# Expert layer of a decoder: picks translated in bf16, a product moved to ScalarE, and other steps for routing and turn

## The reference, cut to what matters

```python
def peer(xn, w_q, sub_keys, u, v):
    q = (xt @ w_q).reshape(T, PEER_HEADS, 2, PEER_HALF)
    s = jnp.einsum('thpc,hpnc->thpn', q, sub_keys).astype(jnp.float32)
    s1, i1 = lax.top_k(s[:, :, 0], PEER_TOPK)
    s2, i2 = lax.top_k(s[:, :, 1], PEER_TOPK)
    cand = (s1[..., :, None] + s2[..., None, :]).reshape(T, PEER_HEADS, PEER_TOPK * PEER_TOPK)
    cidx = (i1[..., :, None] * PEER_N_KEYS + i2[..., None, :]).reshape(T, PEER_HEADS, PEER_TOPK * PEER_TOPK)
    top_s, top_j = lax.top_k(cand, PEER_TOPK)
    expert = jnp.take_along_axis(cidx, top_j, axis=-1)
    gate = jax.nn.softmax(top_s, axis=-1).astype(xn.dtype)
    ...
        h = jax.nn.gelu(jnp.einsum('cd,chkd->chk', xc, u[ec]), approximate=False)
        return jnp.einsum('chk,chkd->cd', gc * h, v[ec])
```

## Time and profile before

| | us |
|---|---|
| median of 3 runs (3453.45 to 3467.33) | 3453.63 |
| profiled execution, its own time | 3456.26 |
| its span | 3454.4 |
| PE busy | 3285.0 (95%) |
| DVE busy | 2666.9 (77%) |
| ACT busy | 1400.3 (41%) |
| POOL busy | 1126.0 (33%) |
| mean granted clock of PE | 0.973 |

### The profile page before, as it was taken

The page is one execution under the profiler, slowest core; times in us unless marked ns, Lnnn a source line. Parts: engine busy times, 40 slices in busy tenths (PEclk is TensorE's granted clock), DMA queues, the critical chain, the costliest instruction groups (busy, mean ns, idle before and its releaser), DMA issues. The chain is left out here.

```text
span 3454.4 us, 49213 instructions
## 1 busy us (share of the span) xinstructions
PE 3285.0 (95%) x18534; PEld 2920.1 (85%) x18534; DVE 2666.9 (77%) x5415; ACT 1400.3 (41%) x2205; POOL 1126.0 (33%) x666
## 2 busy tenths in 40 slices
PE   7988999999999999998999998999999999999997
PEld 6866899999998788886978876799989998788886
DVE  4664799898976888885457875699898976788886
ACT  3333245545453333332435544234545453333332
POOL 1311363423312464450000001354342422466561
PEclk9988999999999999999999998999999999999999
DMA  4102358878889999993222212348888789999995
GB/s 163 62 7 91 123 170 294 290 268 292 274 315 345 389 389 388 379 384 133 96 74 74 74 44 80 122 131 287 286 272 283 274 312 338 392 391 390 388 390 204
DMA packets 324349, 833.65 MB, mean 241 GB/s; under 512 B 26001, under 2 KB 160657, under 8 KB 320017
## 3 DMA queue, kind: packets, MB, share of 16 engines
q1 hardware_dynamic: 250384, 562.04, 46.3%
q0 software_dynamic: 73728, 268.47, 21.4%
HBM read 721.30 MB, written 109.10 MB: 240 GB/s over the span
## 5 line engine op out<-in xcount | busy, mean ns | idle before, releaser
L1959 ACT ACTIVATE peer_hi<-peer_raw 128x1024 fp32r<-128x1024 f32 x540 | 570.5, 1057 | 651.9 <-PE p_bank L1933 358.6
L2173 DVE TENSOR_TENSOR peer_lo<-peer_raw,peer_hi 128x1024 fp32r<-128x1024 f32 x434 | 532.3, 1227 | 339.4 <-ACT peer_hi L1959 339.1
L1862 POOL DMA_INDIRECT p_grow<-in_u_rows,p_expert x256 | 329.6, 1287 | 758.4 <-DVE p_hid L2181 744.3
L1862 POOL DMA_INDIRECT p_grow<-in_v_rows,p_expert x256 | 452.3, 1767 | 362.9 <-DVE p_acc L2190 315.0
L1933 PE MATMUL p_bank<-peer_hi,p_w_hi 128*128 128x512 f32 x1536 | 478.4, 393 | 3.7 <-DVE peer_lo L2173 3.6
L1933 PE MATMUL p_bank<-peer_lo,p_w_hi 128*128 128x512 f32 x1536 | 478.5, 393 | 0.0
L1933 PE MATMUL p_bank<-peer_hi,p_w_lo 128*128 128x512 f32 x1536 | 478.2, 392 | 0.0
L1884 PE MATMUL p0r_h_ps<-peer_x_hi,peer_hi 128*128 128x384 f32 (+1 forms) x1152 | 401.9, 349 | 11.9 <-ACT p_h_sb L1973 6.6
L1884 PE MATMUL p1r_h_ps<-peer_x_hi,peer_hi 128*128 128x384 f32 (+1 forms) x1152 | 401.3, 348 | 10.0 <-ACT p_h_sb L1973 6.5
L1884 PE MATMUL p0r_h_ps<-peer_x_lo,peer_hi 128*128 128x384 f32 (+1 forms) x1152 | 395.4, 343 | 0.0
L1884 PE MATMUL p1r_h_ps<-peer_x_lo,peer_hi 128*128 128x384 f32 (+1 forms) x1152 | 395.1, 343 | 0.0
(11 more groups left out here) (365 smaller groups left out, 5806.5 us busy)
## 6 DMA issues: line engine op xcount, KB each, us to landing
peer_raw<-in_u SPq DMA_DIRECT2D x256, 512.0 KB, 5.0
peer_raw<-in_v SPq DMA_DIRECT2D x256, 512.0 KB, 10.6
hiddens<-p_h_sb SPq DMA_DIRECT2D x256, 192.0 KB, 3.4
p_w_raw<-hiddens SPq DMA_DIRECT2D x64, 768.0 KB, 10.1
p_g_sb<-gates SPq DMA_DIRECT2D x64, 768.0 KB, 14.0
gates<-x SPq DMA_DIRECT2D x12, 2048.0 KB, 9.5
ba_w<-in_w_b_mix SPq DMA_DIRECT2D x38, 512.0 KB, 3.7
peer_raw<-in_w_peer_q SPq DMA_DIRECT2D x32, 512.0 KB, 4.0
```

The lines of the kernel that those rows point to most:

```text
L1862: pool.indirect_dma_start(out=grow[:, g % RG, :], out_offset=None, in_=table, in_offset=bass.IndirectOffsetOnAxis(ap=expert[:, at:at + 1], ...
L1959: act.activation(hi[:, n % NH, :], raw[:, n % NR, :], ACT.Copy).then_inc(hi_ready, 1)
L2173: dve.tensor_tensor(lo[:, m % NH, :], raw[:, m % NR, :], hi[:, m % NH, :].bitcast(F32), ALU.subtract).then_inc(lo_dve, 1)
```

## The change

Four things change in `peer_stage`. The table of picks and its factors become bf16, and are built by one comparison, eight products and a tree of sums for each of the two sides. The product of `same` with the first part of the gates goes from DVE to ACT, eight activations a batch with one token's gate as the scale. That part is kept in fp32 (`piece0`). Routings of tiles 2 and 3 start 33 blocks after the one before, instead of 35. The turn comes one block later behind its routing, the cut and the one-hots as before.

```diff
-    route_step = [LIST_END, LIST_END + 8, LIST_END + 43, LIST_END + 78]
+    route_step = [LIST_END, LIST_END + 8, LIST_END + 41, LIST_END + 74]
...
     def turns_after(t):
-        return route_step[t] + 9
+        return route_step[t] + ROUTE_PIECES + 1
 
     def cut_step(t):
-        return route_step[t] + 10
+        return turns_after(t) + 1
 
     def hot_step(k):
 
-        return route_step[1 + k // TILE_BATCHES] + 11 + (k % TILE_BATCHES) * 7 // 5
+        return cut_step(1 + k // TILE_BATCHES) + (k % TILE_BATCHES) * 7 // 5
...
-            best_f = early.sb("best_f", [P, NQ, TOPK])
-            table = early.sb("table", [P, TOPK * HK])
+            best_b = early.sb("best_b", [P, NQ, TOPK, 2], BF16)
+            place_b = early.sb("place_b", [P, 2, HK], BF16)
+            table = early.sb("table", [P, 2 * HEADS * CANDS])
...
-            hit = table[:, :].rearrange("p (c k) -> p c k", k=HK)
+            hit = table[:, 0:TOPK * HK // 2].bitcast(BF16).rearrange("p (c k) -> p c k", k=HK)
...
                 def place_gates(k):
                     pe.wait_ge(rows_ready, k + 1)
-                    pe.wait_ge(cols_ready, (k + 1) * PIECES)
+                    pe.wait_ge(cols_ready, (k + 1) * (PIECES - 1))
+                    pe.wait_ge(first_cols, k + 1)
...
+                def weigh_columns(k):
+                    if k % TILE_BATCHES == 0:
+                        act.wait_ge(done, k // TILE_BATCHES + 1)
+                    act.wait_ge(equal, k + 1)
+                    if k >= 2:
+
+                        act.wait_ge(multiplied, (k - 1) * BATCH)
+                    for v in range(BATCH):
+                        at = k * BATCH + v
+                        ins = act.activation(cols[:, k % 2, 0, v // 2, :, v % 2], same[:, v // 2, :, v % 2], ACT.Copy,
+                                             scale=piece0[:, at:at + 1])
+                    ins.then_inc(first_cols, 1)
+
...
+                    if n - 1 in hots_at:
+                        weigh_columns(hots_at[n - 1])
                     if n in place_at:
                         move_gates(place_at[n])
...
                     for s in range(2):
-                        place = pos_f[:, 3 * s, :].rearrange("p (h k) -> p h k", k=TOPK)
-                        for c in range(TOPK):
-                            step.mark(dve.scalar_tensor_tensor(
-                                out=hit[:, c, :].rearrange("p (h k) -> p h k", k=TOPK), in0=place, scalar=float(c),
-                                in1=best_f[:, s:NQ:2, c:c + 1].broadcast_to(by_head), op0=ALU.is_equal, op1=ALU.mult))
+                        step(dve.tensor_tensor(hit.rearrange("p c (k b) -> p c k b", b=2),
+                                               place_b[:, s, :].rearrange("p (k b) -> p k b", b=2).unsqueeze(1)
+                                               .broadcast_to(pairs),
+                                               iota2[:, 0:TOPK, :].unsqueeze(2).broadcast_to(pairs), ALU.is_equal))
+                        for a in range(HEADS):
+                            mine = hit[:, :, a * TOPK:(a + 1) * TOPK].rearrange("p c (k b) -> p c k b", b=2)
+                            step.mark(dve.tensor_tensor(
+                                mine, mine, best_b[:, 2 * a + s, :, :].unsqueeze(2).broadcast_to([P, TOPK, TOPK // 2, 2]),
+                                ALU.mult))
                         step.wait()
                         yield
-                        step(dve.tensor_reduce(pick[:, s, :], hit[:, :, :].rearrange("p c k -> p k c"), AX.X, ALU.add))
+                        n = TOPK // 2
+                        while n > 1:
+                            step(dve.tensor_tensor(hit[:, 0:n, :], hit[:, 0:n, :], hit[:, n:2 * n, :], ALU.add))
+                            n //= 2
+                        step(dve.tensor_tensor(pick[:, s, :], hit[:, 0, :], hit[:, 1, :], ALU.add))
...
                     if k:
 
-                        dve.wait_ge(cols_ready, k * PIECES)
+                        dve.wait_ge(cols_ready, k * (PIECES - 1))
+                        dve.wait_ge(first_cols, k)
...
-                    for c in range(PIECES):
-                        dve.tensor_tensor(cols[:, k % 2, c, :, :, :], same[:, :, :, :], per_token(pieces, c, k),
+                    for c in range(PIECES - 1):
+                        dve.tensor_tensor(cols[:, k % 2, c + 1, :, :, :], same[:, :, :, :], per_token(pieces, c, k),
                                           ALU.mult).then_inc(cols_ready, 1)
```

More of the change, by code:

```diff
@@ L1728, in peer_stage @@
             places = early.sb("places", [P, 2, SD], BF16)
-            pieces = early.sb("pieces", [P, PIECES, SD], BF16)
+            piece0 = early.sb("piece0", [P, SD])
+            rounded = early.sb("rounded", [P, P], BF16)
+            pieces = early.sb("pieces", [P, PIECES - 1, SD], BF16)
             qT = early.sb("qT", [P, 2, S])
@@ L1771, in peer_stage @@
          cut, done, equal, rows_ready, cols_ready, multiplied, g_moved, weighted, w_hi_ready, w_lo_ready, x_loaded,
-         xrow_ready, indexed, used, hidden, weighed, added, gain_loaded, x_stored) = [st.sem(s) for s in (
+         xrow_ready, indexed, used, hidden, weighed, added, gain_loaded, x_stored, first_cols) = [st.sem(s) for s in (
              "hi_ready", "lo_pool", "lo_dve", "summed", "taken", "keys_loaded", "scored", "listed", "own", "shift_done",
@@ L2056, in route @@
                 def route(t):
-                    step.mark(dve.tensor_copy(best_f[:, :, :], best_at[:, t, :, :]))
+                    step.mark(dve.tensor_copy(best_b[:, :, :, :],
+                                              best_at[:, t, :, :].unsqueeze(3).broadcast_to([P, NQ, TOPK, 2])))
                     for first, n_a, n_b in ((0, FULL, TOPK), (FULL, TOPK - FULL, FULL)):
@@ L2101, in route @@
                     step(dve.tensor_tensor(pos_f[:, 1, :], pos_f[:, 1, :], flat_f[:, :], ALU.mult))
-                    step.mark(dve.tensor_tensor(pos_f[:, 0, :], pos_f[:, 0, :], pos_f[:, 1, :], ALU.add))
+                    step.mark(dve.tensor_tensor(place_b[:, 0, :], pos_f[:, 0, :], pos_f[:, 1, :], ALU.add))
                     step(dve.tensor_tensor(pos_f[:, 2, :], pos_f[:, 2, :], flat_f[:, :], ALU.mult))
-                    step(dve.tensor_tensor(pos_f[:, 3, :], pos_f[:, 3, :], pos_f[:, 2, :], ALU.add))
+                    step(dve.tensor_tensor(place_b[:, 1, :], pos_f[:, 3, :], pos_f[:, 2, :], ALU.add))
@@ L2135, in cut_gates @@
                     at, gates = slice((t - 1) * P, t * P), t_ps[:, 2 * P:3 * P]
-                    dve.tensor_copy(pieces[:, 0, at], gates).then_inc(cut, 1)
+                    before = (t - 1) * 5
+                    if t > 1:
+                        dve.wait_ge(cut, before)
+                    dve.tensor_copy(rounded[:, :], gates).then_inc(cut, 1)
                     dve.tensor_copy(places[:, :, at], t_ps[:, 0:2 * P].rearrange("p (a b) -> p a b", b=P))\
                         .then_inc(cut, 1)
-                    dve.wait_ge(cut, t * 4 - 2)
-                    dve.tensor_tensor(left[:, :], gates, pieces[:, 0, at], ALU.subtract).then_inc(cut, 1)
-                    dve.wait_ge(cut, t * 4 - 1)
-                    dve.tensor_copy(pieces[:, 1, at], left[:, :]).then_inc(cut, 1)
-                    dve.wait_ge(cut, t * 4)
-                    dve.tensor_tensor(pieces[:, 2, at], left[:, :], pieces[:, 1, at],
+                    dve.wait_ge(cut, before + 2)
+                    dve.tensor_copy(piece0[:, at], rounded[:, :]).then_inc(cut, 1)
+                    dve.tensor_tensor(left[:, :], gates, rounded[:, :], ALU.subtract).then_inc(cut, 1)
+                    dve.wait_ge(cut, before + 4)
+                    dve.tensor_copy(pieces[:, 0, at], left[:, :]).then_inc(cut, 1)
+                    dve.wait_ge(cut, before + 5)
+                    dve.tensor_tensor(pieces[:, 1, at], left[:, :], pieces[:, 0, at],
                                       ALU.subtract).then_inc(done, 1)
```

3 lines of the change are left out of this document (2 added, 1 removed).

## The result

The changed kernel took 3427.78 us, the median of 6 runs (3424.97 to 3437.35). The kernel before, run beside it, took 3460.12 (3453.45 to 3467.33). The ratio is 0.9913, with a 95% interval of 0.9892 to 0.9934: faster by 23 to 37 us. Executions of one kernel differ by 12 to 14 us, so the profiled one of the changed kernel (3435.57 us, span 3433.8) is only 20.6 us shorter in its span than the profiled one of before.

What follows compares the result with a forecast made beforehand. PE, busy 95% of the span, bounds the kernel; only its waits and slow clock can shrink. 26.2 + 7.3 = 33.5, less 1 allowed, gives 32.5 us: 3423.8 as profiled, 3421 median; range 3411 to 3440.

Steps and rivals of the forecast that it cites:

- the 33.5 us that were to go at the turns: PE's chain at the turns: 26.2 us of waits plus 7.3 us of slow-clock blocks behind them were to go.
- The waits on the gate: PE's transposes at the turns wait for a routing's gates, 26.2 us over both expert layers; forecast to end.
- A side: One of a routing's two halves on DVE: new operations 4.8 us instead of 7.17, saving 2.4 a side, 4.8 a routing.
- R2: Rival: ACT's strided activations cost 0.45 us each, ACT becomes the bound, 39 us added, 3460 us; chance 0.10.
- R1: Rival: routing no shorter, POOL's lowerings block the new two-input DVE operations; gain 18 to 26 us, say 3431; chance 0.20.
- With 4.8 us gained and the blocked time unchanged: DVE's routings: with the later turn, all four long waits end 1.7 to 3.7 us before PE comes.
- The waits of tile 1: PE's two waits at tile 1's turns, 1.8 us together, under 1 us each, were to end too.
- Behind the turn are late only the cut of the gates and the first one-hot, in DVE's next block: DVE's queue behind the turn: PE needs these only three blocks further, so the deadline moves the full 4.16 us.
- the spacing and ACT's product at nothing: Routings 33 blocks apart, and DVE's 66 us of products moved to ACT: both costed at no change in time.
- the long waits: PE's four waits at the turns before token tiles 2 and 3: 5.92, 5.25, 5.92 and 7.30 us, all to end.
- R3: Rival: in routings ACT's late take and exponential table loads meet in one block, up to 11.6 us, 3433; chance 0.08.
- The start of the weighing: Moves 4 blocks ahead, same distance to the last store of gates; its stall was to stay as it is.

Runs made afterwards that it cites:

- the split store: Changed kernel with each 2 MB store of gates sent as four 512 KB transfers in four successive blocks: 3431.71 us, 0.9929; same edit on the kernel before: 3455.34 us, 0.9992.

## Why the prediction was right, and where not

The forecast was 32.5 us less; the medians give 32.3, the ratio 30, and the two profiled executions 20.6 in their spans. The size is right and the list of causes is not, since two terms were too large and two that stood at nothing were not. That they made up for each other is luck: the 33.5 us that were to go at the turns are 25.1 in the table (37.2 to 12.1), and without the spacing, which was put at nothing, the gain is 16 us.

*Right.* The waits on the gate went to nothing. A side costs what was forecast where nothing disturbs it: the rest of a routing fell by 4.4 us, against 4.8. ACT's activations take 0.310 us against 0.307, hot blocks keep their pace, and R2 did not come. The Trainium skill, SBUF — State Buffer, section Who interferes with whom, had the side of R1: two-input DVE instructions wait for the whole of a GpSimd instruction that reads SBUF, tensor_reduce does not; the sums of 1.47 us that took 6.28 and the reductions that kept 3.88 agree. In the routing of tile 2 before, only the first reduction had a lowering beneath it (the second starts at 698.03, and the last lowering ends at 694.46), so by that rule 2.4 of the 4.8 us go, and they did.

*Wrong: "With 4.8 us gained and the blocked time unchanged".* Picks save 2.0 us a routing at tiles 2 and 3 (50.9 to 49.0, 50.6 to 48.4), since the blocked time rose by one lowering. This is R1's mechanism at half its price; waits of its size are there, but on DVE's lowering and not at the transposes. The waits of tile 1, which were to end, became longer by the picks. In the whole change they can't be told from nothing: 0.9922 without them, 0.9913 with them, the intervals overlap.

*Wrong: "Behind the turn are late only the cut of the gates and the first one-hot, in DVE's next block".* DVE's own lowering for the block behind the turn stands in the same queue, 3.4 us behind the gate. I listed what is queued behind the gate by the edits and left out the work that DVE does in every block outside a routing. So the deadline moved by some 1.3 us instead of 4.16, and 12.1 us of excess are left at and behind the turns, of 37.2 (some 3 us of either are the six turns' own transposes).

*Wrong: the spacing and ACT's product at nothing.* Picks and turn at their measured size would take 2.0 + 1.3 us from each of the long waits (and bring tails of low clock to an end), and the kernel that has both, with ACT's product, gained 16 us. The other 14 came with the spacing (10 in the excess of the profiled executions), which moves the routing against POOL's lowerings. That it needs ACT's product to start in time is what the rows suggest (a cast 0.6 us later without it); the times, 23 us without it and 30 with it, overlap in their intervals. I had asked of both only whether their own work fits, and not where DVE would stand when the next routing begins.

*R3* came (the take's stall, then the table loads in the next block), but in tile 3's routing alone, with 5.8 us in the two layers together instead of up to 11.6, and cost nothing that can be told: the split store removed it, 3.3 us came back elsewhere, and the median did not get better. The start of the weighing, which I had put at no change, costs 2.7 us more.

The parts don't add. Alone, turn, picks and spacing give 6, 2 and 4 us; left out, they cost 9, 3 and 14 of 30. What stays open: for tile 2 the rows show which lowering the new place covers, but at tile 3 only that the blocked time differs; and whether another distance than 33 is better still was not tried.

## What to carry to other kernels

Before a deadline is moved, list everything that stands in the late engine's queue behind the late result, also the work it does every block, and ask which of it is wanted next; the real deadline is the earliest of these. When two engines exclude each other, the price is the number of the other's instructions times their length, less those that fall under instructions that don't take part: a slow instruction that doesn't take part can be worth as much as a fast one that does. A stall upstream of a wait costs nothing while the wait remains, and an edit that is worth nothing alone can be worth half of the gain beside others, so leave parts out as well as try them alone.
